# First feed-forward layer: gate and up by the two-matmul product with 512 moving columns, its low half copied out of the bank and added

## The chip, the cores and the metric

One core of a Trainium2 chip runs the whole program. The metric is the device time in microseconds (us) of one execution; lower is better. TensorE is called PE below (PEld its weight loads), VectorE DVE, ScalarE ACT, SyncE SP.

## What is computed

The reference runs 256 tokens (plus 16 meta tokens) of width 1024 through one block of retention and attention with a gated feed-forward layer, and then through two further layers, each with a feed-forward layer of squared ReLU. All weights are fp32 and are read once. The change touches the first feed-forward layer alone:

```
h = h + (silu(n @ w_ffn_gate) * (n @ w_ffn_up)) @ w_ffn_down     # n = rmsnorm(h); 1024 -> 2816 -> 1024
```

The later two (`m0` and `m1` below) are `x + square(relu(h @ w1)) @ w2`, 1024 -> 4096 -> 1024.

## The kernel before, in words

**Number format.** TensorE works on fp32r operands. For accuracy each fp32 operand is split in two parts, hi and lo: ACT writes the hi part of a weight chunk (`whi`, line 1195), DVE subtracts it from the raw chunk and writes the lo part (`wlo`, the `split` of the vector engine, through the helper `tt` at line 1667). A product is then hi·hi + hi·lo + lo·hi. The activations `u` and `v` have the parts as index 0 and 1 of their second dimension.

**Two ways to multiply.** `split_mm` (line 451) gives three matmuls of 256 moving columns for each of the kt = 8 slices of the contraction: whi by u-hi, whi by u-lo, wlo by u-hi, all summed in the same 256 columns of a PSUM bank. `split_wide` (lines 460 and 461) gives two: wlo by u-hi with 256 columns, and whi by both parts of u side by side, 512 columns in one instruction. Then whi by u-lo is summed in the right half of the bank and has to be added to the left half by another engine. Before the change `m0` and `m1` use `split_wide`, and `ffn` uses `split_mm`.

**The stream of weights.** Weights come in chunks of up to 2048 columns into a ring of 4 buffers (`raw`, `whi`, `wlo`). SP loads chunk n once DVE has split chunk n-4 (`lo_ready`). ACT splits chunk n (`hi_ready`) once it has landed and PE has used chunk n-4 (`chunk_used`), DVE follows, PE waits for `lo_ready`. ACT and DVE split three chunks ahead of the one in hand (`AHEAD = 3`).

**The ffn layer.** The hidden width 2816 is cut in 22 steps of 128, k = 0 to 21. A step has an A chunk (gate and up columns of this step, 2 x 1024 columns of a buffer) and a B chunk (128 rows of `w_ffn_down`, 1024 columns). The order on every engine is written out by hand, in `hidden_layer` of each engine's program; k = 1 to 20 run in a hardware loop with two steps in a turn:

- PE: up(0), up(1), down(0), up(2), down(1), ..., up(21), down(20), down(21). `up` (line 889 on) waits for `lo_ready` of its A chunk and for `hidden_val` of step k-2, writes gate and up of the step into two banks of `proj`, and posts `chunk_used`. `down` (line 912) waits for the B chunk and for `hidden_ready` of its own step, and sums into `aux`.
- DVE, for a step k: [split of B chunk k, 1024 columns: wlo] then wait for `chunk_used` of up(k), gate times rms and up times rms/2 (two operations `f<-proj,r_all`, the first posts `ffn_gate_scaled`), wait for `ffn_gate_tanh`, (tanh + 1) times gate (line 1670), times up (`f<-f`, posts `hidden_val`), wait for `hidden_hi`, subtract for the lo part (`v<-f,v`, posts `hidden_ready`), then [split of A chunk k+2, 2048 columns], [split of B chunk k+1], and the next step.
- ACT, for a step k: wait for `ffn_gate_scaled`, tanh (line 1447), wait for `hidden_val`, copy to v-hi (line 1450, posts `hidden_hi`), split of A chunk k+2, split of B chunk k+1 (line 1195).

Every operation of DVE and ACT posts a semaphore for which the engine itself waits before it goes on (`Lane.post` and `Lane.run`), so an engine takes its list strictly in order. In `m0` and `m1` the same list has three more things in a step: ACT first waits for `chunk_used` and copies the right halves of both banks to SBUF (line 1438, `low_kept`), and DVE waits for `low_kept` and adds (`f<-proj,f`, 128x512).

Of the kernel before, what the change touches and what calls it, by code (L numbers as in the profile page):

```python
# [11 lines left out]
P = 128  # L12
# [176 lines left out]
def build(nc, w, params, consts, late, ln_gb, out):  # L189
# [11 lines left out]
    with ExitStack() as ctx:  # L201
# [47 lines left out]
        def W(part, n, off, kt, cols):  # L249

            t = (whi, wlo)[part]
            return t[:, n % RING, off:off + kt * cols].rearrange("p (k n) -> p k n", k=kt)
# [188 lines left out]
        def _(pe):  # L441
# [440 lines left out]
            def hidden_layer(d, norm_no):  # L882
                tag, n_h, kt, k0 = d["tag"], d["n"], d["kt"], d["k0"]
                g = loop_first[tag]
                turn = bank_turn[tag]

                def up(n, k, i=None, gate=None, between=None):
                    pe.wait_ge(sems["lo_ready"], at(lambda m: m + 1, n, i))
                    if k0 + k >= 2:

                        pe.wait_ge(sems["hidden_val"], k0 + k - 1 if i is None else i * 2 + (k0 + k - 1))
                    for j in range(2):
                        first_gate = gate if j == 0 else None
                        if tag == "ffn":
                            ins = split_mm(proj[:, 2 * ((k + turn) % 2) + j, 0:S], lambda a, q: W(a, n, 1024 * j, KT, P)[:, q, :],
                                           lambda a, q: u[:, a, q, META:L], KT, gate=first_gate)
                        else:
                            ins = split_wide(proj[:, 2 * ((k + turn) % 2) + j, :], lambda a, q: W(a, n, 0, KT, 256)[:, q, j * P:(j + 1) * P],
                                           lambda a, q: u[:, a, q, META:L], KT, gate=first_gate)
                        if between and j == 0:  # L900
                            between()
                    finish(ins)

                def down(n, k, i=None, first=False, last=False):
                    pe.wait_ge(sems["lo_ready"], at(lambda m: m + 1, n, i))
                    pe.wait_ge(sems["hidden_ready"], k0 + k + 1 if i is None else i * 2 + (k0 + k + 1))
                    for q in range(kt):
                        for j in range(8):
                            ins = None
                            for s, (a, b) in enumerate(((0, 0), (0, 1), (1, 0))):  # L910

                                ins = mm(aux[:, j // 2, (j % 2) * S:(j % 2 + 1) * S],  # L912
                                         W(a, n, 0, kt, D)[:, q, j * P:(j + 1) * P], v[:, b, 2 * (k % 2) + q, :],
                                         start=first and q == 0 and s == 0 and j % 2 == 0,
                                         stop=last and q == kt - 1 and s == 2, skip_group_check=True)
                            if last and q == kt - 1 and j in (1, 3, 5):
                                ins.then_inc(sems["down_bank"], 1)
                    finish(ins)


                def turn_residual():

                    for k in range(KT):
                        for b in range(2):
                            mm(aux[:, 2 * b + k // 4, (k % 4) * P:(k % 4 + 1) * P], x2[:, k, b * P:(b + 1) * P], C("ident"),
                               start=k % 4 == 0, stop=False, skip_group_check=True)

                def down_tokens(n, k, i=None, last=False):
                    pe.wait_ge(sems["lo_ready"], at(lambda m: m + 1, n, i))
                    pe.wait_ge(sems["hidden_ready"], k0 + k + 1 if i is None else i * 2 + (k0 + k + 1))  # L930
                    for c in range(4):
                        for q in range(kt):
                            for s, (a, b) in enumerate(((0, 0), (0, 1), (1, 0))):
                                ins = mm(aux[:, c, :], v[:, b, 2 * (k % 2) + q, c // 2 * P:(c // 2 + 1) * P],  # L934
                                         W(a, n, 0, kt, D)[:, q, c % 2 * 512:(c % 2 + 1) * 512], start=False,
                                         stop=last and q == kt - 1 and s == 2, skip_group_check=True)
                        if last and c < 3:
                            ins.then_inc(sems["down_bank"], 1)
                    finish(ins)

                pe.wait_ge(sems["proj_free"], order[g - 1])
                up(g, 0, gate=by_half(norm_no), between=lambda: whole_sum(norm_no))
                pe.wait_ge(sems["proj_free"], order[g - 1] + 1)
                up(g + 1, 1)
                pe.wait_ge(sems["rms_ready"], norm_no + 1)
                if tag == "m1":
                    turn_residual()
                    down_tokens(g + 2, 0)
                else:
                    down(g + 2, 0, first=True)  # L950
                add_down = down_tokens if tag == "m1" else down
                with pe.Fori(0, (n_h - 2) // 2) as i:
                    up(g + 3, 2, i)
                    add_down(g + 4, 1, i)
                    up(g + 5, 3, i)
                    add_down(g + 6, 2, i)
                add_down(g + 2 * n_h - 1, n_h - 1, last=True)
# [221 lines left out]
        def _(eng):  # L1179
# [242 lines left out]
            def hidden_layer(d):  # L1422
# [3 lines left out]
                def step(n, k, i=None):  # L1426
# [5 lines left out]
                    if k is None:  # L1432
                        return
                    kk = (lambda c: k0 + k + c if i is None else i * 2 + (k0 + k + c))
                    if tag != "ffn":
                        b = 2 * ((k + bank_turn[tag]) % 2)
                        eng.wait_ge(sems["chunk_used"], at(lambda m: m + 1, n, i))
                        A.post(act(f("f1", 1024, 2, S), proj[:, b:b + 2, S:2 * S], ACT.Copy), "low_kept")  # L1438

                    def buffer_free():  # L1440

# [14 lines left out]
                step(g, 0)  # L1456
                turns = (n_h - 2) // 2
                with eng.Fori(0, turns) as i:
                    A.enter(i, {"hi_ready": 4, "low_kept": 0 if tag == "ffn" else 2, "hidden_hi": 2, "ffn_gate_tanh": 2 if tag == "ffn" else 0})
                    step(g + 1, 1, i)  # L1460
                    step(g + 2, None, i)
                    step(g + 3, 2, i)
                    step(g + 4, None, i)
# [196 lines left out]
        def _(eng):  # L1660
# [390 lines left out]
            def hidden_layer(d, no, gain=None, norm_no=None):  # L2051
# [3 lines left out]
                def step(n, k, i=None):  # L2055
# [7 lines left out]
                    kk = (lambda c: k0 + k + c if i is None else i * 2 + (k0 + k + c))  # L2063
                    eng.wait_ge(sems["chunk_used"], at(lambda m: m + 1, n, i))
                    b, slot = 2 * ((k + bank_turn[tag]) % 2), 2 * (k % 2)
                    if tag == "ffn":
                        g0, hid, up = f("f1", 0, S), f("f1", 256, S), f("f1", 512, S)
                        B.post(tt(g0, proj[:, b, 0:S], rms, ALU.mult), "ffn_gate_scaled")
                        B.run(tt(up, proj[:, b + 1, 0:S], half_rms, ALU.mult))
                        eng.wait_ge(sems["ffn_gate_tanh"], kk(1))  # L2070
                        B.run(stt(g0, proj[:, b, 0:S], 1.0, g0, ALU.add, ALU.mult))
                        B.post(tt(hid, g0, up, ALU.mult), "hidden_val")
                        eng.wait_ge(sems["hidden_hi"], kk(1))
                        B.post(tt(v[:, 1, slot, :], hid, hi32(v[:, 0, slot, :]), ALU.subtract), "hidden_ready")
                    else:
                        rl, hid, both = f("f1", 0, 2, S), f("f1", 512, 2, S), f("f1", 1536, 2, S)
                        eng.wait_ge(sems["low_kept"], kk(1) - M0["k0"])
                        B.run(tt(both, proj[:, b:b + 2, 0:S], f("f1", 1024, 2, S), ALU.add))
                        B.run(stt(rl, both, 0.0, bc(rms, 2), ALU.max, ALU.mult))
                        B.post(tt(hid, rl, rl, ALU.mult), "hidden_val")  # L2080
                        eng.wait_ge(sems["hidden_hi"], kk(1))
                        B.post(tt(v[:, 1, slot:slot + 2, :], hid, hi32(v[:, 0, slot:slot + 2, :]), ALU.subtract), "hidden_ready")
# [3 lines left out]
                step(g, 0)  # L2086
                turns = (n_h - 2) // 2
                with eng.Fori(0, turns) as i:
                    B.enter(i, {"lo_ready": 4, "hidden_val": 2, "hidden_ready": 2, "dve_step": 4,
                                "ffn_gate_scaled": 2 if tag == "ffn" else 0})  # L2090
                    step(g + 1, 1, i)
                    step(g + 2, None, i)
                    step(g + 3, 2, i)
                    step(g + 4, None, i)
# [400 lines left out]
```

## Time and profile before

| what | value |
|---|---|
| runs | 1081.0 us median of 3 (1079.75 to 1083.07) |
| profiled execution, span from first to last instruction | 1076.7 us |
| what lies around the span, against the median | 4.3 us |
| PE busy / PEld busy / DVE busy / ACT busy | 1057.1 / 979.9 / 747.6 / 547.2 us |
| ffn layer in the trace | up(1) starts at 287.7, last `down` starts at 467.6 us |

The profiled execution's own time outside the profiler isn't listed; the 4.3 us are the median of the runs less the span. A PE row's duration is longer than the distance to the next row, since matmuls are pipelined: read the distance of starts. "idle before <-" names what ended an engine's wait.

### The profile page before, as it was taken

The numbers are of one execution on the slowest core, as the hardware profiler recorded it, in microseconds if no ns is written. First come the engines' busy times: TensorE is split into PE (matmuls) and PEld (weight loads), VectorE is DVE, ScalarE is ACT, GpSimd is POOL, SyncE is SP. The second block draws the span as 40 slices with busy tenths as digits, with TensorE's granted clock in tenths as the row PEclk, the third lists the DMA queues.
The fourth block names the chain that finished last, engine by engine and source line by source line (L and its number), as shares of the span: only waits on it lengthen the run. The fifth ranks groups of instructions, "written<-read, shape, count | busy, mean of one in ns | idle before, by whom it ended". The sixth has DMA issues, their size and how long they took to land.

```text
span 1076.7 us, 19451 instructions
## 1 busy us (share of the span) xinstructions
PE 1057.1 (98%) x7774; PEld 979.9 (91%) x7774; DVE 747.6 (69%) x810; ACT 547.2 (51%) x587; POOL 2.2 (0%) x5
## 2 busy tenths in 40 slices
PE   8999999999999999999999999999999999999998
PEld 7998897999999999989989999999999998888887
DVE  6855748768766766677767766666679987666673
ACT  6423536554644444455786444343566574354442
POOL 0000000000000000000000000000000000000000
PEclk9999999999999999999999999999999999999999
DMA  9883243336556556746316564654354454655531
GB/s 308 229 225 118 79 142 100 126 124 194 158 170 200 176 176 191 237 150 202 117 46 230 162 228 156 205 185 135 101 160 154 141 173 157 211 180 183 207 117 39
DMA packets 162589, 177.37 MB, mean 165 GB/s; under 512 B 4800, under 2 KB 148288, under 8 KB 162536
## 3 DMA queue, kind: packets, MB, share of 16 engines
q1 hardware_dynamic: 160704, 174.33, 50.5%
q10 hardware_dynamic: 1832, 2.30, 1.2%
q8 instruction: 38, 0.62, 0.2%
q14 instruction: 15, 0.12, 0.0%
HBM read 175.04 MB, written 1.57 MB: 164 GB/s over the span
## 4 chain that ended last, share of the span: by engine, by line
PE 76%; DVE 16%; ACT 4%; DMA 1%; issue 1%; ACTq 1%; SPq 0%; DVEq 0%
PE proj L451 32%; PE aux L912 13%; PE proj L461 10%; PE aux L934 8%; DVE wlo L1667 6%; PE proj L460 5%; DVE f L1667 3%; DVE f L1670 2%; ACT whi L1195 1%; DMA gamma_rows<-f 1%; DVE u L1670 1%; PE aux L665 1%; PE aux L518 1%; PE aux L780 1%; PE aux L765 1%
## 5 line engine op out<-in xcount | busy, mean ns | idle before, releaser
L1667 DVE TENSOR_TENSOR wlo<-raw,whi 128x2048 fp32r<-128x2048 f32 (+2 forms) x179 | 374.7, 2093 | 113.0 <-ACT whi L1195 101.3
L451 PE MATMUL proj<-u,whi 128*128 128x256 f32 (+1 forms) x1888 | 347.2, 285 | 2.7 <-DVE f L1667 1.6
L1195 ACT ACTIVATE whi<-raw 128x2048 fp32r<-128x2048 f32 (+2 forms) x173 | 309.7, 1790 | 70.7 <-PE proj L451 29.4
L451 PEld LDWEIGHTS proj<-u,whi 128*128 128x128 f32 x1888 | 292.9, 190 | 8.8 <-issue 6.5
L451 PE MATMUL proj<-u,wlo 128*128 128x256 f32 (+1 forms) x944 | 267.1, 283 | 0.0
L461 PE MATMUL proj<-u,whi 128*128 128x512 f32 x512 | 179.9, 393 | 0.0
L451 PEld LDWEIGHTS proj<-u,wlo 128*128 128x128 f32 x944 | 179.3, 190 | 0.0
L912 PE MATMUL aux<-v,whi 128*128 128x256 f32 x864 | 155.2, 281 | 1.8 <-DVE v L1667 1.8
L460 PE MATMUL proj<-u,wlo 128*128 128x256 f32 x512 | 143.6, 281 | 0.9 <-DVE u L1670 0.9
L912 PEld LDWEIGHTS aux<-v,whi 128*128 128x128 f32 x864 | 133.3, 189 | 3.0 <-issue 2.3
L912 PE MATMUL aux<-v,wlo 128*128 128x256 f32 x432 | 121.1, 280 | 0.0
L461 PEld LDWEIGHTS proj<-u,whi 128*128 128x128 f32 x512 | 96.1, 188 | 20.9
L451 PE MATMUL proj<-v,whi 128*128 128x256 f32 (+1 forms) x564 | 103.1, 284 | 0.6 <-DVE f L1667 0.5
L460 PEld LDWEIGHTS proj<-u,wlo 128*128 128x128 f32 x512 | 96.4, 188 | 3.3 <-DVE u L1670 1.4
L451 PEld LDWEIGHTS proj<-v,whi 128*128 128x128 f32 x564 | 87.1, 189 | 2.9 <-issue 2.1
L912 PEld LDWEIGHTS aux<-v,wlo 128*128 128x128 f32 x432 | 81.5, 189 | 0.0
L934 PE MATMUL aux<-whi,v 128*128 128x512 f32 x256 | 80.1, 394 | 0.0
L451 PE MATMUL proj<-v,wlo 128*128 128x256 f32 (+1 forms) x282 | 79.5, 282 | 0.0
L1438 ACT ACTIVATE f<-proj 128x512 f32<-128x512 f32 x32 | 19.1, 598 | 98.3 <-PE proj L461 98.1
L1667 DVE TENSOR_TENSOR f<-proj,r_all 128x256 f32<-128x256 f32 (+5 forms) x85 | 46.4, 545 | 30.9 <-PE proj L451 26.7
L451 PE MATMUL proj<-whi,u 128*128 128x256 f32 (+1 forms) x352 | 65.1, 280 | 1.1 <-DVE f L1673 0.6
L1454 ACT ACTIVATE v<-f 128x512 fp32r<-128x512 f32 x32 | 20.3, 634 | 79.2 <-DVE f L1667 75.2
(302 smaller groups left out, 1092.2 us busy)
## 6 DMA issues: line engine op xcount, KB each, us to landing
raw<-in_mlp_w_dram SPq DMA_DIRECT2D x64, 1024.0 KB, 5.5
raw<-in_w_in_dram SPq DMA_DIRECT2D x21, 1024.0 KB, 7.1
raw<-in_od_w_in_dram SPq DMA_DIRECT2D x12, 1024.0 KB, 5.5
raw<-in_w_ffn_gate_dram SPq DMA_DIRECT2D x22, 512.0 KB, 4.0
raw<-in_w_ffn_up_dram SPq DMA_DIRECT2D x22, 512.0 KB, 5.2
raw<-in_w_ffn_down_dram SPq DMA_DIRECT2D x21, 512.0 KB, 5.4
raw<-in_ev_w_in_dram SPq DMA_DIRECT2D x10, 1024.0 KB, 6.1
raw<-in_w_ret_out_dram SPq DMA_DIRECT2D x4, 1024.0 KB, 5.2
```

Of the source, the lines that this page charges most:

```text
L451: ins = mm(o, w_of(a, k), x_of(b, k), start=first and k == 0 and j == 0, stop=last and k == kt - 1 and j == 2, skip_group_check=skip)
L460: mm(bank[:, 0:S], w_of(1, k), x_of(0, k), start=k == 0, stop=False, skip_group_check=True)
L461: ins = mm(bank, w_of(0, k), x_of(slice(0, 2), k), start=False, stop=k == kt - 1, skip_group_check=True)
L518: ins = mm(aux[:, 0, 0:tokens], weights, sq_of(tokens)[:, k, :], start=k == 0, stop=k == KT - 1, skip_group_check=True)
L665: ins = mm(out[e], rv_tok[:, 1 - j, h * P:(h + 1) * P], sd[:, e, j, :], start=False, stop=j == 1)
L912: ins = mm(aux[:, j // 2, (j % 2) * S:(j % 2 + 1) * S], W(a, n, 0, kt, D)[:, q, j * P:(j + 1) * P], v[:, b, 2 * (k % 2) + q, :], start=fir ...
L934: ins = mm(aux[:, c, :], v[:, b, 2 * (k % 2) + q, c // 2 * P:(c // 2 + 1) * P], W(a, n, 0, kt, D)[:, q, c % 2 * 512:(c % 2 + 1) * 512], st ...
L1195: A.post(act(whi[:, n % RING, 0:wd], raw[:, n % RING, 0:wd], ACT.Copy), "hi_ready")
L1438: A.post(act(f("f1", 1024, 2, S), proj[:, b:b + 2, S:2 * S], ACT.Copy), "low_kept")
L1454: A.post(act(v[:, 0, 2 * (k % 2):2 * (k % 2) + 2, :], f("f1", 512, 2, S), ACT.Copy), "hidden_hi")
L1667: return ve.tensor_tensor(o, a, b, op)
L1670: return ve.scalar_tensor_tensor(out=o, in0=a, scalar=s, in1=b, op0=op0, op1=op1)
```

## The change

In `hidden_layer` of PE, ffn's gate and up now go through `split_wide` as well, with the same weight chunks in the same places. ACT copies the right halves of both banks to SBUF in every step of ffn too, ahead of tanh, and waits for `chunk_used` ahead of that. DVE adds left half and copy (128x512) ahead of the scaling, which then reads the sum in SBUF in place of the bank. The loop's tables of semaphore counts follow, and the wait of m0 and m1 for `low_kept` counts ffn's 22 posts as well.

```diff
@@ PE, up @@
                     for j in range(2):
                         first_gate = gate if j == 0 else None
-                        if tag == "ffn":
-                            ins = split_mm(proj[:, 2 * ((k + turn) % 2) + j, 0:S], lambda a, q: W(a, n, 1024 * j, KT, P)[:, q, :],
-                                           lambda a, q: u[:, a, q, META:L], KT, gate=first_gate)
-                        else:
-                            ins = split_wide(proj[:, 2 * ((k + turn) % 2) + j, :], lambda a, q: W(a, n, 0, KT, 256)[:, q, j * P:(j + 1) * P],
-                                           lambda a, q: u[:, a, q, META:L], KT, gate=first_gate)
+                        def rows_of(a, q):
+                            if tag == "ffn":
+                                return W(a, n, 1024 * j, KT, P)[:, q, :]
+                            return W(a, n, 0, KT, 256)[:, q, j * P:(j + 1) * P]
+
+                        ins = split_wide(proj[:, 2 * ((k + turn) % 2) + j, :], rows_of, lambda a, q: u[:, a, q, META:L], KT,
+                                         gate=first_gate)
@@ ACT, hidden_layer @@
-                    if tag != "ffn":
-                        b = 2 * ((k + bank_turn[tag]) % 2)
-                        eng.wait_ge(sems["chunk_used"], at(lambda m: m + 1, n, i))
-                        A.post(act(f("f1", 1024, 2, S), proj[:, b:b + 2, S:2 * S], ACT.Copy), "low_kept")
+                    b = 2 * ((k + bank_turn[tag]) % 2)
+                    eng.wait_ge(sems["chunk_used"], at(lambda m: m + 1, n, i))
+                    A.post(act(f("f1", 1024, 2, S), proj[:, b:b + 2, S:2 * S], ACT.Copy), "low_kept")
@@ DVE, hidden_layer @@
                     eng.wait_ge(sems["chunk_used"], at(lambda m: m + 1, n, i))
                     b, slot = 2 * ((k + bank_turn[tag]) % 2), 2 * (k % 2)
+                    both = f("f1", 1536, 2, S)
+                    eng.wait_ge(sems["low_kept"], kk(1))
+                    B.run(tt(both, proj[:, b:b + 2, 0:S], f("f1", 1024, 2, S), ALU.add))
                     if tag == "ffn":
                         g0, hid, up = f("f1", 0, S), f("f1", 256, S), f("f1", 512, S)
-                        B.post(tt(g0, proj[:, b, 0:S], rms, ALU.mult), "ffn_gate_scaled")
-                        B.run(tt(up, proj[:, b + 1, 0:S], half_rms, ALU.mult))
+                        B.post(tt(g0, both[:, 0], rms, ALU.mult), "ffn_gate_scaled")
+                        B.run(tt(up, both[:, 1], half_rms, ALU.mult))
                         eng.wait_ge(sems["ffn_gate_tanh"], kk(1))
                         ...
                     else:
-                        rl, hid, both = f("f1", 0, 2, S), f("f1", 512, 2, S), f("f1", 1536, 2, S)
-                        eng.wait_ge(sems["low_kept"], kk(1) - M0["k0"])
-                        B.run(tt(both, proj[:, b:b + 2, 0:S], f("f1", 1024, 2, S), ALU.add))
+                        rl, hid = f("f1", 0, 2, S), f("f1", 512, 2, S)
```

## Rows read from the trace of the kernel before

**Rows 1.** The page, part 1: busy us (share of the span) x instructions

```profile
PE 1057.1 (98%) x7774; PEld 979.9 (91%) x7774; DVE 747.6 (69%) x810; ACT 547.2 (51%) x587; POOL 2.2 (0%) x5
```

**Rows 2.** Chain that ended last, in order of time (start, us, what), ffn

```profile
304.69 5.66 PE proj L451 x48
...
310.35 2.83 PE aux L912 x24
313.18 5.68 PE proj L451 x48
```

**Rows 3.** The same chain in m0, two neighbouring steps

```profile
630.18 5.70 PE aux L912 x48
641.46 5.70 PE aux L912 x48
```

**Rows 4.** Busy by stretch, the middle of ffn; then granted clock and DMA

```profile
295.00:455.00 160.00, 160.00 (x1358) 160.00 (x1357) 107.40 (x134) 71.96 (x76) 0.00 (x0) 1.00 0.63 188
```

**Rows 5.** Timeline of DVE, two steps of ffn (start, us, ..., idle before)

```profile
360.71 1.22 DVE L1667 TENSOR_TENSOR wlo<-raw,whi 128x1024 fp32r<-128x1024 f32 x1 [0.38 <-DVE wlo L1667]
362.06 0.88 DVE L1667 TENSOR_TENSOR f<-proj,r_all 128x256 f32<-128x256 f32 x2
...
366.53 3.64 DVE L1667 TENSOR_TENSOR wlo<-raw,whi 128x2048 fp32r<-128x2048 f32 x2 [1.61 <-ACT whi L1195]
370.30 0.88 DVE L1667 TENSOR_TENSOR f<-proj,r_all 128x256 f32<-128x256 f32 x2
...
378.79 0.88 DVE L1667 TENSOR_TENSOR f<-proj,r_all 128x256 f32<-128x256 f32 x2
```

**Rows 6.** Timeline of ACT, the first of these steps

```profile
362.52 0.39 ACT L1447 ACTIVATE proj<-f 128x256 f32<-128x256 f32 x1 [2.93 <-DVE f L1667]
...
364.58 1.92 ACT L1195 ACTIVATE whi<-raw 128x2048 fp32r<-128x2048 f32 x1 [0.19 <-ACT v L1450]
366.68 1.06 ACT L1195 ACTIVATE whi<-raw 128x1024 fp32r<-128x1024 f32 x1 [0.18 <-ACT whi L1195]
```

**Rows 7.** Waits within ffn, 284 to 468 us (in total, times, longest)

```profile
DVE wlo L1667 <- ACT whi L1195: 33.0, 21, 1.6
...
PE aux L912 <- DVE v L1667: 1.4, 1, 1.4
DVE f L1667 <- PE proj L451: 1.4, 4, 0.4
```

**Rows 8.** Timeline of ACT, then of DVE, one step of m0

```profile
641.50 0.60 ACT L1438 ACTIVATE f<-proj 128x512 f32<-128x512 f32 x1 [3.54 <-PE proj L461]
...
642.13 0.69 DVE L1667 TENSOR_TENSOR f<-proj,f 128x512 f32<-128x512 f32 x1 [1.48 <-ACT f L1438]
642.85 0.69 DVE L1670 SCALAR_TENSOR_TENSOR f<-f,r_all 128x512 f32<-128x512 f32 x1
```

**Rows 9.** Timelines of DVE and ACT at the start of ffn

```profile
289.96 0.88 DVE L1667 TENSOR_TENSOR f<-proj,r_all 128x256 f32<-128x256 f32 x2
...
295.12 0.89 DVE L1667 TENSOR_TENSOR f<-proj,r_all 128x256 f32<-128x256 f32 x2
...
299.60 3.64 DVE L1667 TENSOR_TENSOR wlo<-raw,whi 128x2048 fp32r<-128x2048 f32 x2 [1.61 <-ACT whi L1195]
...
288.67 0.20 ACT L1208 ACTIVATE small<-small 128x1 f32<-128x1 f32 x1
```

**Rows 10.** Timeline of DVE at the end of ffn

```profile
454.85 0.88 DVE L1667 TENSOR_TENSOR f<-proj,r_all 128x256 f32<-128x256 f32 x2 [0.39 <-PE proj L451]
...
464.51 0.88 DVE L1667 TENSOR_TENSOR f<-proj,r_all 128x256 f32<-128x256 f32 x2
...
467.00 0.42 DVE L1667 TENSOR_TENSOR v<-f,v 128x256 fp32r<-128x256 f32 x1 [0.60 <-ACT v L1450]
```

**Rows 11.** Timeline of DVE, the product of gate and up, operands in SBUF

```profile
363.47 0.43 DVE L1667 TENSOR_TENSOR f<-f 128x256 f32<-128x256 f32 x1
```

**Rows 12.** Timeline of PE, and busy by stretch, at the start of the program

```profile
10.04 1.13 PE L574 MATMUL proj<-cst,f 128*128 128x128 f32 x6 [1.90 <-DMA f<-in_x_dram]
...
12.00:14.00 2.00, 2.00 (x10) 1.87 (x10) 1.86 (x5) 1.77 (x3) 0.00 (x0) 0.50 1.11 350
```

More of the change, by code:

```diff
@@ L1458, in hidden_layer @@
                 with eng.Fori(0, turns) as i:
-                    A.enter(i, {"hi_ready": 4, "low_kept": 0 if tag == "ffn" else 2, "hidden_hi": 2, "ffn_gate_tanh": 2 if tag == "ffn" else 0})
+                    A.enter(i, {"hi_ready": 4, "low_kept": 2, "hidden_hi": 2, "ffn_gate_tanh": 2 if tag == "ffn" else 0})
                     step(g + 1, 1, i)
@@ L2088, in hidden_layer @@
                 with eng.Fori(0, turns) as i:
-                    B.enter(i, {"lo_ready": 4, "hidden_val": 2, "hidden_ready": 2, "dve_step": 4,
+                    B.enter(i, {"lo_ready": 4, "hidden_val": 2, "hidden_ready": 2, "dve_step": 6 if tag == "ffn" else 4,
                                 "ffn_gate_scaled": 2 if tag == "ffn" else 0})
```

## The prediction, made before the changed kernel was run

> **What bounds the kernel now.** The page's first part comes first: PE is busy for 98% of the span, DVE for 69%, ACT for 51% [rows 1]. Taken alone it says that only PE counts. The stretch in question has to be read by itself, and by its period rather than by busy time. In the chain of waits ffn is a steady alternation of up (48 matmuls, 5.68 us) and down (24, 2.83 us), 8.51 us a step [rows 2]; from 295 to 455 us PE is busy for all of 160 us [rows 4]. So PE is the bound there before.
>
> The second thing to read is how far behind PE the other two engines run. Take DVE in the same stretch and measure from one scaling of the gate to the next: 362.06 to 370.30 is 8.24 us, 370.30 to 378.79 is 8.49 us [rows 5] (the second has the jump back of the hardware loop, with 0.38 us idle before its wlo). Neither start shows a wait for PE. What sets them is a ring through two engines, whose links follow at once on one another: gate scaled at 362.06, tanh on ACT at 362.52, copy to v, then ACT's 2048-column split at 364.58 [rows 6], then DVE's two lo splits from 366.53 to 370.17, then the next gate at 370.30 [rows 5]. DVE has 1.61 us idle in it, and ACT 2.93, but both idle times lie inside the ring: DVE waits for a split that ACT may start only after tanh and the copy, since ACT works its list in order. The ring turns in 16.73 us for two steps, 8.37 a step, against PE's 8.51. **Its slack is 0.14 us a step, though DVE is busy for only two thirds of the time.** The waits confirm it: DVE waited for up of PE only 4 times in 22 steps, 1.4 us in all, longest 0.4 [rows 7]; it began the layer late and only caught up near its end. At the end PE waits 1.4 us for the last v [rows 7].
>
> **The change, part by part.**
>
> *PE.* Each up has 32 matmuls and weight loads where it had 48, for the same 768 columns a slice. m0 has this form: from one down to the next is 641.46 - 630.18 = 11.28 us, less the down's 5.70, leaves 5.58 for its up of the same size [rows 3], against 5.68 [rows 2]. That is 0.10 us a step, 2.2 us over 22 steps, and a PE period of 8.41. It counts only while PE is the bound.
>
> *ACT.* One copy of 128x512 from PSUM in each step, 0.60 us [rows 8], and a wait for chunk_used ahead of it, with tanh, the copy to v and two splits queued behind. Its place is the idle time before tanh: ACT ends its 1024-column split at 366.68 + 1.06 = 367.74, and tanh of the next step can't start before the next gate is scaled, about 370.7 [rows 5, 6]. The copy can start when up(k) is done. DVE is going to fall behind PE (below), so up(k) is then long done, and the copy is over before DVE asks. I cost it at nothing; its cover is those 2.93 us, and if PE ended its up last, the copy would be in series: 0.63 us a step with the hand-over (641.50 to 642.13 [rows 8]). In step 0 ACT is free at 288.87 and DVE scales at 289.96 [rows 9], which just holds a copy of 0.60.
>
> *DVE.* One addition of 128x512 of a bank and SBUF ahead of the gate's scaling: m0 has the same operation, 0.69 us, and the next starts 0.73 us (642.85 - 642.13, rounded up) after it [rows 8]. It lies in the ring, nothing covers it. The wait for low_kept costs nothing where the copy is done; one more wait that has passed already I bound by 0 and 0.1 us a step (the gap of 0.13 from the end of wlo to the gate [rows 5] has one), and take 0.
>
> *The scalings* read the sum in SBUF in place of the bank. A product of two SBUF operands of 128x256 takes 0.43 us [rows 11], a pair of scalings out of the bank 0.88 [rows 5]: no difference, so I take 0. The Trainium skill (VectorE: DVE Perf Modes, the section on the TRN2 errata) has a fixed term of 58 cycles for an SBUF source and 120 for PSUM, which by its 0.96 GHz would be an estimated 0.065 us less for the gate's link, 1.4 us over the layer. By it the sum below would be 13.8; the rows show none of it, and the sum goes by the rows.
>
> *The sum.* With the addition the ring is 16.73 + 2 x 0.73 = 18.19 us for two steps, 9.10 a step: longer than PE's 8.41. The bound changes hands. What counts now is the ring from its first to its last link, and before it also ran nearly unhindered: gate(0) at 289.96, gate(20) at 454.85, gate(21) at 464.51 [rows 9, 10]. So all 22 additions go onto the end of the layer, 22 x 0.73 = 16.1 us, less what DVE spent waiting for PE: 1.4 us in 4 times [rows 7], less the 0.13 that stand before each gate anyway, about 0.9. **The last v comes 15.2 us later, at about 482.6 in place of 467.4** [rows 10]. PE's 2.2 us are hidden in its waits. A check from PE's side: the lo split of A chunk 3 ends at 299.60 + 2.29 = 301.9 for an up that starts at 304.69 [rows 2, 9], a lead of 2.8; minus the 1.46 of two additions and 0.3 of faster ups, about 1 us is left, and each step eats 9.10 - 8.41 = 0.69. From the third step on PE waits for wlo some 0.7 us a step, 17 times, about 12 us; at the end down(20) is over about 7.2 us before the last v (it was 1.4). 12 + (7.2 - 1.4) - 2.2 gives 15.6, the same within my rounding.
>
> *After the layer* everything hangs on that v (residual, norm, next projections), and the splits that ACT and DVE do ahead there are in the same lists, so they shift along. SP, its loads and the later layers are unchanged but for the count they wait for. I count no recovery.
>
> *The clock.* The wait of 7.2 us is longer than any in the trace before. There PE idled 1.90 us at 8.1 to 10.0 us, and after it the granted clock was 0.50 of full, the 1.2 GHz level, from 12 to 14 us [rows 12]. The 1.4 us at the end of ffn had no such trace. So I expect the last down and what follows it to start at half clock. Priced from those rows: 10 matmuls in 2 us, 0.20 each, against 0.118 at full clock (2.83 over 24 [rows 2]) is 0.08 lost on each. I don't know how many will be slow; for 10 to 16 it is 0.8 to 1.3 us. Part of it may hide behind DVE's residual additions, so the bounds are 0.6 and 1.3, and I take 1.0. The Trainium skill (TensorE: Matmul & The Clock Gate, on what is actually happening) says that an idle array falls to 1.2 GHz and regains 2.4 by activity; that speaks for this case.
>
> Sum: 15.2 + 1.0 = 16.2 on the profiled span of 1076.7, 1092.9 with 4.3 us around it: against the median **1081.0 + 16.2 = 1097.2 us**.
>
> **The rivals.**
> - *No fall of the clock:* 1081.0 + 15.2 = 1096.2. The same in all else. Chance 0.33.
> - *PE stays the bound, not slower:* the Trainium skill (Perfetto Trace Analysis, the section on the most-contended engine) says to improve the most occupied engine first, and that is PE, at 98%. The mechanism here would be that DVE's 1.61 us of idle time absorb the 0.73: ACT's split would have to be ready earlier. Then only the 2.2 us count: 1081.0 - 2.2 = 1078.8, too little to tell from no change (about 0.3%, 3.2 us, is what a measurement of this kernel can). It decides at a ring of 8.41 us: for more than 0.04 us of addition the ring loses. Against it: the 21 waits of wlo for ACT [rows 7] follow at once upon ACT's own end [rows 6]. Chance 0.05: 0.03 for this, and 0.02 for more than 3.2 us faster, should PE gain at the layer's end as well.
> - *Copy and addition both in series:* 22 x 0.63 = 13.9 more, 1111. It needs PE's up to end last in each step, which a ring slower than PE excludes. Chance 0.04.
> - *Partly absorbed:* the ring has slack that I don't see (the hardware loop's 0.38 us taken up by the longer step, the skill's cheaper SBUF source): 10 x 0.25 + 1.4, about 4 less, 1092 to 1093. Chance 0.08.
>
> **How the numbers follow.** The forecast's own case has 0.47, and its range goes from 1095.5 to 1099.5 (the wait at 0.1 us a step gives 2.2 on top of it, the clock 0.6 to 1.3). The range with the neighbours is 1092.5 to 1100; outside lie PE as the bound, the series case and 0.03 for what I haven't thought of (0.02 of it no change, 0.01 faster), under 0.2 together. Slower by over 0.3%: 0.47 + 0.33 + 0.04 + 0.08 = 0.92; within: 0.03 + 0.02 = 0.05; faster: 0.02 + 0.01 = 0.03.
>
> **What would show it.** Right: gates 9.0 to 9.2 us apart on DVE; no wait of DVE for up of PE or for the copy after the first steps; PE waits of about 0.7 us for wlo in most steps and one of about 7 us for the last v, and DVE the same 1.6 us for ACT; up at 5.6 us where PE doesn't wait; the last v near 482.6; a clock under 1 shortly after. Wrong: a period near 8.4 with PE busy throughout (the ring had slack), a period near 9.7 with DVE waiting for ACT's copy (the copy is in the ring), or a shift at the end of ffn that has shrunk by the end of the program (the later stages had room).

## The result and the profile after

The changed kernel took 1099.8 us (median of 4 runs, 1098.9 to 1100.9) where the kernel before took 1081.4 beside it. The ratio of the runs is 1.0183, with a 95% interval of 1.0166 to 1.0201: slower by about 1.8%, 18.4 us by the medians and 19.8 by the ratio. The prediction was 1097.2 with a range up to 1100.0; by the ratio the kernel comes out at 1100.8, so the direction and the ring as the bound were right and the size fell short by 2.6 to 3.6 us.

The span of the profiled execution went from 1076.7 to 1097.2, 20.5 us. Not all of that is the change: the two executions differ by 1.3 us before ffn begins. DVE's reciprocal at the layer's start stands at 285.52 before and at 286.82 after; already the PE work at 10.04 that waits for a part of the input [rows 12] starts at 10.33, and in the other profiled executions below the reciprocal stands anywhere from 285.3 to 288.0. So from here on I measure **the stretch**: from this reciprocal to the start of the last `v` of ffn (a), and to the reciprocal of the next norm (b), which takes in what follows the layer. Before, (a) is 467.00 - 285.52 = 181.48 and (b) is 480.72 - 285.52 = 195.20. The changed kernel and two runs below that should have the same ring give 200.08, 200.05 and 200.13 for (a), so a few tenths of a microsecond in it can be read. The first part of the page, and the kinds of wait within ffn, after:

The page, part 1:

```profile
PE 1062.6 (97%) x7422; PEld 967.5 (88%) x7422; DVE 762.7 (70%) x832; ACT 560.3 (51%) x609; POOL 2.2 (0%) x5
```

The waits within 284 to 490 us (in total, times, longest), kernel after:

```profile
DVE wlo L1667 <- ACT whi L1196: 31.3, 21, 1.6
...
DVE v L1667 <- ACT v L1450: 14.6, 22, 1.0
PE proj L460 <- DVE wlo L1667: 10.0, 16, 0.8
...
PE aux L913 <- DVE v L1667: 7.2, 2, 6.7
...
DVE wlo L1667 <- DVE wlo L1667: 4.9, 10, 0.6
DVE f L1667 <- DVE wlo L1667: 4.3, 20, 0.2
```

PE has 352 matmuls fewer (22 x 16), and waits where it did not: 16 times for the lo split of a chunk, 10 us, and 6.7 us for the last v. In [rows 7] its only wait was the last, 1.4. DVE's waits for up have vanished from the list, and DVE doesn't wait for ACT's copy in it either. DVE's busy share rose by one point only, 69% to 70%: no share of busy time says what happened here.

Two steps in the same places of the loop's body as in [rows 5] (steps 3 and 4, there 9 and 10), with the addition of step 2 ahead of them. DVE's timeline after, and under it ACT's for step 3 (start, us, ..., idle before):

```profile
306.34 0.69 DVE L1667 TENSOR_TENSOR f<-proj,f 128x512 f32<-128x512 f32 x1 [0.21 <-DVE wlo L1667]
...
315.88 0.69 DVE L1667 TENSOR_TENSOR f<-proj,f 128x512 f32<-128x512 f32 x1 [0.22 <-DVE wlo L1667]
316.60 0.89 DVE L1667 TENSOR_TENSOR f<-f,r_all 128x256 f32<-128x256 f32 x2
...
319.10 0.43 DVE L1667 TENSOR_TENSOR v<-f,v 128x256 fp32r<-128x256 f32 x1 [0.60 <-ACT v L1450]
321.12 3.64 DVE L1667 TENSOR_TENSOR wlo<-raw,whi 128x2048 fp32r<-128x2048 f32 x2 [1.59 <-ACT whi L1196]
324.97 0.69 DVE L1667 TENSOR_TENSOR f<-proj,f 128x512 f32<-128x512 f32 x1 [0.21 <-DVE wlo L1667]
```

```profile
312.11 1.06 ACT L1196 ACTIVATE whi<-raw 128x1024 fp32r<-128x1024 f32 x1 [0.57 <-PE proj L461]
313.29 0.60 ACT L1438 ACTIVATE f<-proj 128x512 f32<-128x512 f32 x1
317.12 0.39 ACT L1447 ACTIVATE proj<-f 128x256 f32<-128x256 f32 x1 [3.24 <-DVE f L1667]
```

Read them with the ring in mind. The copy at 313.29 is over at 313.89, 2 us before DVE adds: it is covered. The addition at 315.88 has nothing before it but wlo, so it isn't. And three small links have grown: 0.21 to 0.22 us between wlo and the addition, where 0.13 stood before the scaling; (not shown) 0.52 to 0.57 in the jump of the hardware loop, where 0.38 to 0.40 stood; and from the start of the gate's scaling to the start of tanh, 316.60 to 317.12, it is 0.52 us, where 362.06 to 362.52 [rows 5, 6] was 0.46. From addition to addition over two steps, 306.34 to 324.97, are 18.63 us (18.58 from the third turn of the loop on); the sum had 18.19, and before it was 16.73.

The end of the layer, DVE and then PE:

```profile
481.36 2.29 DVE L1667 TENSOR_TENSOR wlo<-raw,whi 128x2048 fp32r<-128x2048 f32 x1 [0.21 <-DVE wlo L1667]
483.69 0.69 DVE L1667 TENSOR_TENSOR f<-proj,f 128x512 f32<-128x512 f32 x1
...
486.90 0.42 DVE L1667 TENSOR_TENSOR v<-f,v 128x256 fp32r<-128x256 f32 x1 [0.60 <-ACT v L1450]
489.20 0.69 DVE L1667 TENSOR_TENSOR x_all<-x_all,aux 128x512 f32<-128x512 f32 x1 [1.87 <-PE aux L913]
```

```profile
487.48 0.76 PE L913 MATMUL aux<-v,whi 128*128 128x256 f32 x2 [6.68 <-DVE v L1667]
```

Stretch (a) is 486.90 - 286.82 = 200.08, which is 18.6 more than before, and (b) 214.49, 19.3 more. The difference between the two, 0.7, is put down to the clock (tried below). Busy time by stretch (PE, PEld, DVE, ACT, POOL, then the granted clock, DMA share and GB/s):

```profile
482.00:484.00 2.00, 0.00 (x0) 0.00 (x0) 1.97 (x2) 0.00 (x0) 0.00 (x0) 1.00 0.75 242
484.00:486.00 2.00, 0.00 (x0) 0.00 (x0) 1.77 (x5) 0.39 (x1) 0.00 (x0) 1.00 1.09 371
486.00:488.00 2.00, 0.53 (x2) 0.56 (x3) 0.73 (x2) 1.60 (x2) 0.00 (x0) 0.51 1.10 349
488.00:490.00 2.00, 2.00 (x12) 2.00 (x11) 0.69 (x1) 0.33 (x3) 0.00 (x0) 0.50 0.28 87
490.00:492.00 2.00, 2.00 (x11) 2.00 (x11) 1.45 (x3) 1.90 (x4) 0.00 (x0) 0.50 0.00 0
```

The clock is at 1.2 GHz (0.50) when the last down begins, at 487.48.

### The profile page after: what moved, and what is told of

The parts are those of the page before. It is cut to its first block, busy times and chain, and to the rows that moved or that the text cites. A ratio compares the mean times of both kernels' runs of the same rounds, so it can differ in the third digit from the quotient of the medians.

```text
span 1097.2 us, 18797 instructions
## 1 busy us (share of the span) xinstructions
PE 1062.6 (97%) x7422; PEld 967.5 (88%) x7422; DVE 762.7 (70%) x832; ACT 560.3 (51%) x609; POOL 2.2 (0%) x5
## 4 chain that ended last, share of the span: by engine, by line
PE 61%; DVE 24%; ACT 9%; issue 3%; DMA 2%; ACTq 1%; DVEq 0%; SPq 0%
PE proj L451 21%; DVE wlo L1667 12%; PE proj L461 10%; PE aux L913 9%; PE aux L935 8%; DVE f L1667 6%; PE proj L460 5%; ACT whi L1196 5%; DVE f L1670 3%; DMA gamma_rows<-f 1%; ACT v L1450 1%; ACT proj L1447 1%; PE aux L665 1%; PE aux L518 1%; PE aux L780 1%
## 5 line engine op out<-in xcount | busy, mean ns | idle before, releaser
L461 PE MATMUL proj<-u,whi 128*128 128x512 f32 x864 | 303.5, 393 | 0.0
L460 PE MATMUL proj<-u,wlo 128*128 128x256 f32 x864 | 244.1, 282 | 11.1 <-DVE wlo L1667 10.0
L451 PE MATMUL proj<-u,whi 128*128 128x256 f32 (+2 forms) x1184 | 222.2, 289 | 1.9 <-DVE f L1667 1.6
L461 PEld LDWEIGHTS proj<-u,whi 128*128 128x128 f32 x864 | 162.3, 188 | 34.9
L451 PEld LDWEIGHTS proj<-u,whi 128*128 128x128 f32 (+1 forms) x1184 | 186.2, 192 | 6.4 <-issue 5.4
L460 PEld LDWEIGHTS proj<-u,wlo 128*128 128x128 f32 x864 | 162.6, 188 | 17.7 <-DVE wlo L1667 8.0
L451 PE MATMUL proj<-u,wlo 128*128 128x256 f32 (+2 forms) x592 | 168.8, 285 | 0.0
L451 PEld LDWEIGHTS proj<-u,wlo 128*128 128x128 f32 (+1 forms) x592 | 113.4, 192 | 0.0
L1438 ACT ACTIVATE f<-proj 128x512 f32<-128x512 f32 x54 | 32.3, 598 | 99.3 <-PE proj L461 96.8
L1667 DVE TENSOR_TENSOR f<-proj,f 128x512 f32<-128x512 f32 x54 | 37.3, 692 | 46.5 <-ACT f L1438 41.2
```

What stands on the lines that cost most here:

```text
L451: ins = mm(o, w_of(a, k), x_of(b, k), start=first and k == 0 and j == 0, stop=last and k == kt - 1 and j == 2, skip_group_check=skip)
L460: mm(bank[:, 0:S], w_of(1, k), x_of(0, k), start=k == 0, stop=False, skip_group_check=True)
L461: ins = mm(bank, w_of(0, k), x_of(slice(0, 2), k), start=False, stop=k == kt - 1, skip_group_check=True)
L1667: return ve.tensor_tensor(o, a, b, op)
```

## The experiments

Theory 1, the prediction's: a ring through DVE and ACT (scaling, tanh, product, copy to v, ACT's split of the next A chunk, DVE's two splits) sets ffn's period, the addition lies in it, PE's saving and ACT's copy don't. The rivals: the wide product costs PE time; ACT's copy is on the path; DVE has too much work. Each ratio is to executions of the kernel before on the same chip; the runs stood on more than one chip, so compare ratios or stretches across rows, and not medians. (a) and (b) are from each run's one profile.

| run | median us | ratio to before, 95% | (a) us | (b) us |
|---|---|---|---|---|
| kernel before | | 1 | 181.48 | 195.20 |
| changed kernel | 1099.8 | 1.0183 (1.0166 to 1.0201) | 200.08 | 214.49 |
| PE part alone | 1079.2 | 1.0000 (0.9987 to 1.0013) | 180.48 | 194.88 |
| ACT and DVE part alone | 1100.2 | 1.0195 (1.0182 to 1.0208) | 200.05 | 214.45 |
| ACT's split first | 1083.6 | 1.0039 (1.0026 to 1.0052) | 182.64 | 197.04 |
| before, ACT's split first | 1080.2 | 1.0002 (0.9993 to 1.0012) | 181.57 | 195.30 |
| no second wait | 1098.0 | 1.0188 (1.0166 to 1.0210) | 198.37 | 212.79 |
| half addition | 1093.2 | 1.0132 (1.0117 to 1.0147) | 194.25 | 208.66 |
| copy twice | 1101.9 | 1.0194 (1.0177 to 1.0211) | 200.44 | 214.86 |
| array kept busy | 1100.2 | 1.0198 (1.0183 to 1.0213) | 200.13 | 213.90 |
| split first, peeled | 1080.7 | 1.0001 (0.9985 to 1.0017) | 180.71 | 194.82 |
| the same, next split late | 1079.2 | 0.9988 (0.9976 to 0.9999) | 180.49 | 195.39 |
| before, peeled | 1080.0 | 1.0007 (0.9992 to 1.0022) | 180.37 | 194.11 |

**PE's part alone.** In the kernel before, PE's part of the diff and nothing else.

```diff
-                        if tag == "ffn":
-                            ins = split_mm(proj[:, 2 * ((k + turn) % 2) + j, 0:S], ...)
+                        ins = split_wide(proj[:, 2 * ((k + turn) % 2) + j, :], rows_of, lambda a, q: u[:, a, q, META:L], KT,
+                                         gate=first_gate)
```

> The kernel before with only TensorE's part of the change in ffn: the two-matmul product, without ACT's copy and DVE's addition. Left out of the computation: the products of the hi weights with the lo activations of gate and up (they lie unread in the banks' right halves). Theory 1 (a ring through ACT and DVE sets the period): the ring stays at 8.37 us a step and PE comes to 8.41, so 0.5 to 2.5 us faster than the kernel before, 1079 to 1081. Theory 2 (the wide product itself costs PE time, part of the 18 to 20 us): slower than before by several us.

Ratio 1.0000, stretch (a) 1.0 shorter. The wide product costs nothing: theory 2 falls. It gives nearly nothing either. The ring at 8.37 was only just below PE's 8.51, and now it is the ring that holds: the gates stand 8.22 to 8.24 and 8.48 to 8.51 us apart to the end of the loop. And of the 1.0 us stretch (b) keeps only 0.3, since after PE's longer wait at the end the clock is at half here too (0.50 from 468 to 470 us; (b) less (a) is 14.40 as in the changed kernel, before 13.72). In the waits of this run DVE no longer waits for PE and still waits 33.0 us for ACT's split, while PE's last wait has grown from 1.4 to 2.5:

```profile
DVE wlo L1668 <- ACT whi L1196: 33.0, 21, 1.6
...
PE aux L913 <- DVE v L1668: 2.5, 1, 2.5
```

**ACT's and DVE's part alone.** The changed kernel with `split_mm` on PE again, and the copy from the left halves:

```diff
-                    A.post(act(f("f1", 1024, 2, S), proj[:, b:b + 2, S:2 * S], ACT.Copy), "low_kept")
+                    A.post(act(f("f1", 1024, 2, S), proj[:, b:b + 2, 0:S] if tag == "ffn" else proj[:, b:b + 2, S:2 * S], ACT.Copy), "low_kept")
```

> The changed kernel with TensorE's old three-matmul product in ffn; ACT copies the banks' left halves (the right ones are not written) and DVE adds them. The computation is changed thereby: gate and up come out doubled. Theory 1: within 1 us of the changed kernel, 18 to 20 us slower than before, since PE's 2.2 us are hidden. Theory 2: near the kernel before.

Stretch (a) is 200.05 against 200.08: the whole slowdown without any of PE's part, and PE's 2.2 us are hidden in its waits.

**How the addition counts, and the copy.** Two runs change one length each:

```diff
 half addition, DVE:
+                    if tag == "ffn":
+                        B.run(tt(both[:, 0], proj[:, b, 0:S], f("f1", 1024, S), ALU.add))
...
-                        B.run(tt(up, both[:, 1], half_rms, ALU.mult))
+                        B.run(tt(up, proj[:, b + 1, 0:S], half_rms, ALU.mult))
 copy twice, ACT:
+                    if tag == "ffn":
+                        A.run(act(f("f1", 1024, 2, S), proj[:, b:b + 2, S:2 * S], ACT.Copy))
                     A.post(act(f("f1", 1024, 2, S), proj[:, b:b + 2, S:2 * S], ACT.Copy), "low_kept")
```

> The changed kernel, DVE adds the low sums of gate alone (128x256 in place of 128x512); up is scaled out of its bank. Left out of the computation: up's products of hi weights with lo activations. Ring theory: the link is 0.43 in place of 0.69 us, 22 x 0.27 = 5.8 us less than the changed kernel, stretch about 194.3. Rival (a fixed cost of an extra instruction or wait makes the slowdown, not its length): no or little change.

Stretch 194.25, expected 194.3: an addition that is 0.27 us shorter takes 5.8 us off 22 steps. DVE's rows in this run, where the half addition takes 0.42 to 0.43 us:

```profile
351.07 0.42 DVE L1667 TENSOR_TENSOR f<-proj,f 128x256 f32<-128x256 f32 x1 [0.22 <-DVE wlo L1667]
351.53 0.43 DVE L1667 TENSOR_TENSOR f<-f,r_all 128x256 f32<-128x256 f32 x1
351.99 0.42 DVE L1667 TENSOR_TENSOR f<-proj,r_all 128x256 f32<-128x256 f32 x1
```

They answer the question of the source for the duration of a scaling: out of SBUF (351.53) and out of the bank (351.99) it differs by nothing that counts. The hand-over from the gate's scaling to tanh is another matter: it is 0.52 us in this run too.

> The changed kernel, ACT does its copy twice in each ffn step. Ring theory: ACT has over 3 us idle there, the second copy ends before DVE asks: within 1 us of the changed kernel. Rival (the copy is on the path): 0.6 us a step, 13 us slower than the changed kernel.

The second copy adds 22 x 0.63 = 13.9 us to ACT's list and 0.36 us to the stretch. The run's own executions differ (1096.9 to 1106.1), but its ratio agrees with that of the changed kernel within both intervals. ACT's rows show both copies and 2.6 us of idle time still behind them:

```profile
351.64 0.60 ACT L1439 ACTIVATE f<-proj 128x512 f32<-128x512 f32 x1
352.27 0.60 ACT L1440 ACTIVATE f<-proj 128x512 f32<-128x512 f32 x1
355.48 0.39 ACT L1449 ACTIVATE proj<-f 128x256 f32<-128x256 f32 x1 [2.61 <-DVE f L1669]
```

**What the sum left out.** 3.4 us of the 18.6 in stretch (a) aren't in the 15.2. One candidate is DVE's second wait ahead of the addition:

```diff
-                    eng.wait_ge(sems["chunk_used"], at(lambda m: m + 1, n, i))
+                    if tag != "ffn":
+                        eng.wait_ge(sems["chunk_used"], at(lambda m: m + 1, n, i))
```

> The changed kernel without DVE's own wait for chunk_used of up(k) in ffn (its wait for low_kept covers it, since ACT waits for chunk_used before the copy). Theory 1a (each wait of DVE costs time in the ring even where it has passed, about 0.09 us): the gap between wlo and the addition falls from 0.21 to about 0.13, 22 x 0.09 = 2 us less than the changed kernel, and the layer's stretch from the reciprocal to the last v falls from 200.1 to about 198. Theory 1b (a passed wait is free and the extra 3.4 us of the stretch are something else): no change.

The stretch falls by 1.71 us, and the addition follows wlo at 360.66, 0.12 after its end, where 0.21 stood:

```profile
356.90 3.64 DVE L1667 TENSOR_TENSOR wlo<-raw,whi 128x2048 fp32r<-128x2048 f32 x2 [1.59 <-ACT whi L1196]
360.66 0.69 DVE L1667 TENSOR_TENSOR f<-proj,f 128x512 f32<-128x512 f32 x1
...
368.70 1.23 DVE L1667 TENSOR_TENSOR wlo<-raw,whi 128x1024 fp32r<-128x1024 f32 x1 [0.52 <-DVE wlo L1667]
```

By the ratios alone (1.0188 and 1.0183) this couldn't be told; the stretch tells it. The cost belongs to the loop: in step 21, which stands behind it, the split ends at 481.36 + 2.29 = 483.65 and the addition starts at 483.69, 0.04 later with both waits in between. Inside the loop a wait's count is worked out from the number of the turn, outside it is a constant; whether that makes the difference I didn't try.

The rest is in DVE's rows. Between one wlo and the next, at the jump of the loop and behind its last turn, DVE was idle 4.0 us in 10 times before and 4.9 after. Nine jumps back grew from 0.38 to 0.40 us each to 0.52 to 0.57, and the gap behind the last turn shrank from 0.57 to 0.21. That is 0.9 us together. The waits and the last of these splits before:

```profile
DVE wlo L1667 <- DVE wlo L1667: 4.0, 10, 0.6
```

```profile
462.18 2.29 DVE L1667 TENSOR_TENSOR wlo<-raw,whi 128x2048 fp32r<-128x2048 f32 x1 [0.57 <-DVE wlo L1667]
```

(Those of after stand above.) The later start of tanh gives 1.1 us: the gaps from the second scaling to the operation that needs tanh add up to 1.62 us before and 2.75 after. The two waits for ACT that follow, for v-hi and for the split, are 0.3 us less. 16.1 - 0.9 + 1.7 + 0.9 + 1.1 - 0.3 = 18.6, the whole. Why the jump got longer (DVE has one operation more in each half of the loop's body; without the second wait it is 0.52 as well), and why tanh starts later, stays open. Tanh's 0.52 us isn't simply the addition's doing: in the kernel before, steps 0 and 21, which stand outside the loop, have 0.51 to 0.52 as well.

**The clock.** In the changed kernel PE gets work for its wait:

```diff
+                if tag == "ffn":
+                    pe.wait_ge(sems["hidden_val"], k0 + n_h - 1)
+                    pe.wait_ge(sems["lo_ready"], g + 2 * n_h)
+                    for _ in range(27):
+                        mm(proj[:, 2 * ((n_h - 2 + turn) % 2), :], W(0, g + 2 * n_h - 1, 0, kt, D)[:, 0, 0:P],
+                           u[:, 0:2, 0, META:L], start=True, stop=True, skip_group_check=True)
                 add_down(g + 2 * n_h - 1, n_h - 1, last=True)
```

> The changed kernel, with 27 matmuls of 512 columns added before ffn's last down, into two banks' halves that nobody reads, in the 6.7 us in which PE waits. Nothing of the result changes. Clock theory: the granted clock stays at 1.00 over the wait, the last down runs at full clock, the residual additions start 0.5 us sooner after the last v, and the whole is 0.5 to 1.3 us faster than the changed kernel. Rival (the matmuls after the wait are off the path anyway): no change beyond 0.3 us.

The profile shows what was expected: the clock stays at 1.00, the first residual addition comes 1.65 us after the last v's start in place of 2.30, and (b) less (a) is 13.77 in place of 14.41, before 13.72.

```profile
479.81 6.44 PE L962 MATMUL proj<-u,whi 128*128 128x512 f32 x27 [0.51 <-DVE wlo L1673]
```

```profile
484.00:486.00 2.00, 2.00 (x10) 1.54 (x9) 1.21 (x3) 1.08 (x2) 0.00 (x0) 1.00 1.10 350
486.00:488.00 2.00, 2.00 (x19) 2.00 (x18) 0.90 (x2) 0.98 (x3) 0.00 (x0) 1.00 0.51 159
```

So the half clock costs 0.65 us here, of 1.0 that I took (slightly more, since the added matmuls end late: the last down starts 0.67 us after v, where it was 0.58). The runs don't show it (ratios 1.0198 and 1.0183, intervals of 0.15 to 0.18% to either side): it is too small for them, and that the whole gets faster, as expected, isn't shown.

**Breaking the ring.** No work is removed, ACT only does the split of A chunk k+2 ahead of step k's copy, tanh and v, as soon as up(k) is done:

```diff
 ACT, step():
                     if i is not None:
-                        split(n + AHEAD, i)
+                        if tag != "ffn" or k is not None:
+                            split(n + AHEAD, i)
+                        if tag == "ffn" and k is not None:
+                            split(n + 1 + AHEAD, i)
```

> The changed kernel, ACT's order in ffn changed: the split of A chunk k+2 stands ahead of step k's own copy, tanh and copy to v, in place of behind them. No work is added or removed. Theory 1: the link from tanh over the copy to v to ACT's split to DVE's split is gone, DVE's 1.6 us of waiting for ACT go, the ring is under 8.41, PE is the bound again: 1078.5 to 1080.5, faster than both. Rival (DVE has too much work in a step, or ACT's copy is on the path): stays over 1090.

> The kernel before with the same order of ACT. Theory 1: PE was the bound already, only the late start of DVE and the wait at the layer's end can shrink: 0 to 1.5 us faster than before. Rival: if the order helps by itself, apart from the addition, it gains as much here as in the changed kernel (some 20 us).

By the ratios 1.44 of the 1.83% are back, 15.6 us, and by stretch (a) 17.4 of the 18.6 us, with DVE's work unchanged: it isn't the amount of work but its order. The same order does nothing for the kernel before (1.0002), where the ring wasn't the bound. DVE's timeline in the changed kernel with ACT's split first:

```profile
352.95 3.64 DVE L1670 TENSOR_TENSOR wlo<-raw,whi 128x2048 fp32r<-128x2048 f32 x2
357.59 0.69 DVE L1670 TENSOR_TENSOR f<-proj,f 128x512 f32<-128x512 f32 x1 [1.00 <-ACT f L1441]
...
364.28 1.23 DVE L1670 TENSOR_TENSOR wlo<-raw,whi 128x1024 fp32r<-128x1024 f32 x1 [0.52 <-DVE wlo L1670]
365.98 0.69 DVE L1670 TENSOR_TENSOR f<-proj,f 128x512 f32<-128x512 f32 x1 [0.47 <-ACT f L1441]
```

wlo no longer waits for ACT (the 1.6 us are gone); DVE waits for the copy, thus for PE. From 357.59 to 449.98 are 11 steps of 8.40 us, PE's period with the wide product, 0.11 below the 8.51 of before: this is PE's saving, seen at last. The expectation was still missed: 1083.6 and not 1078.5 to 1080.5. I had priced the steady steps and not the end. The new order puts ACT's split in front of the copy, so the addition starts 2.6 us after PE is through with a step's up. PE covers that while it has further steps, but not at the end: up(20) is over at 455.8, the addition of step 20 starts at 458.39, and that of step 21 at 467.09, behind two 2048-column splits in DVE's list. PE then waits 3.9 us for v, with half clock afterwards (0.50 from 472 to 476 us).

```profile
455.81 1.92 ACT L1196 ACTIVATE whi<-raw 128x2048 fp32r<-128x2048 f32 x1 [1.46 <-PE proj L461]
457.76 0.60 ACT L1441 ACTIVATE f<-proj 128x512 f32<-128x512 f32 x1
```

In stretch (b) this is 1.8 us more than before; the ratio says 4.2 (2.8 at the low end of its interval), and no stretch shows where the rest lies.

Three more runs looked at the end. The first two have ACT's split first and are without DVE's second wait; the third is the kernel before with the last turn written out and nothing else. On ACT and DVE the last turn of ffn's loop is written out, so that the last B chunk is split at its own 1024 columns (in the loop it gets the width of an A chunk), and in the second of them DVE does step 21 ahead of the next stage's first split:

```diff
-                turns = (n_h - 2) // 2
+                turns = (n_h - 2) // 2 - (tag == "ffn")
...
+                if tag == "ffn":
+                    m = g + 1 + 4 * turns
+                    step(m, n_h - 3)
+                    step(m + 1, None)
+                    step(m + 2, n_h - 2)
+                    step(m + 3, None)
                 pump(g + 2 * n_h - 3)
                 step(g + 2 * n_h - 3, n_h - 1)
```

> The changed kernel with ACT's split ahead of the step's chain, without DVE's second wait, and with the last turn of ffn's hardware loop written out on ACT and DVE, so that the last B chunk is split at its own 1024 columns (in the loop it has the width of an A chunk, 2048). Ring theory, where the end of the layer is what is left: DVE's chain of step 21 starts 1.07 us sooner than with the split first alone, stretch about 181.5 (182.6 there), the whole about 1 us faster than it, 1082 to 1083; still not faster than the kernel before, whose stretch is 181.5. Rival (something other than the end of the layer holds the last 3.6 us): unchanged.

> As split_first_peeled, and DVE does its chain of step 21 ahead of the lo split of the first chunk of the next stage (before, behind it). The last v comes about 1.2 us sooner still, stretch about 180.3, but the split then stands between it and the residual additions: these start 2.7 us after the last v in place of 2.3. Whole: 0 to 1 us faster than split_first_peeled, within 1 us of the kernel before.

> The kernel before with the last loop turn of ffn written out on ACT and DVE alone. DVE's chain of step 21 waits for the second 2048-column split until 464.5 though PE's up is done at 463.4: 0.9 us can be gained, stretch about 180.6, whole 0.5 to 1 us faster than before, at the edge of what can be measured.

Peeling, with the second wait left out, takes 1.9 us off stretch (a) of the version with ACT's split first (1.1 expected) and the whole to 1.0001 of the kernel before (1080.7 us, where 1082 to 1083 was expected). All of it is gained at the end: measured from the reciprocal, the addition of step 18 stands at 153.92 and 153.90 us in the two versions, that of step 20 at 170.72 and 170.00, that of step 21 at 179.42 and 177.50. What held the last few us was the end of the layer; how the 1.9 us divide between the narrower split, the second wait and the jump that is no more, this run doesn't tell. Doing the next split late shortens (a) by another 0.2 only (1.2 expected) and lengthens (b) by 0.6, as the split then stands before the residual additions:

```profile
468.26 2.29 DVE L1676 TENSOR_TENSOR wlo<-raw,whi 128x2048 fp32r<-128x2048 f32 x1
470.59 1.41 DVE L1676 TENSOR_TENSOR x_all<-x_all,aux 128x512 f32<-128x512 f32 x2
```

Its ratio, 0.9988 with 0.9999 as the interval's end, is just below one, but its stretch (b) is 0.2 us longer than before's: the 1.0 us that it saves up to the last v is spent again ahead of the next norm. So I don't call it faster. The kernel before, peeled, has both stretches 1.1 us shorter (0.9 expected), and the runs don't resolve it (1.0007). **No version here beats the kernel before by more than 0.3%**; the changed one with ACT's split first and the end peeled equals it.

## Why the prediction came out as it did

- *What bounds the kernel:* right. The ring of 8.37 us, with 0.14 us a step of slack beneath a PE that is busy all the time, is what the order experiment breaks up, and the period goes from 9.29 back to 8.40 us a step.
- *PE's part:* right, 0.10 us a step (0.11 measured where PE is the bound) and wholly hidden: 200.05 without it, 200.08 with it.
- *ACT's copy at nothing:* right, 0.36 us for a second one in all 22 steps.
- *The addition at 0.73 us, 22 times:* right; its length counts one for one (5.8 us for 0.27 a step).
- *The scalings at nothing:* right for their duration, by the rows at 351.53 and 351.99, but not for the link that hangs on them (below). The 1.4 us estimated from the figures of the Trainium skill (VectorE: DVE Perf Modes, the TRN2 errata) don't appear: in this case the duration of a tensor_tensor of 128x256 is the same from SBUF and from the bank.
- *The waits of PE:* 16 for wlo, 10.0 us, expected 17 and about 12; 6.7 us at the end, expected 7.2.
- ***The step that failed:*** the ring's new period was the old one plus the addition and nothing else, 18.19 us for two steps; it measured 18.58 to 18.63. The term that was mis-sized is "one more wait that has passed already I bound by 0 and 0.1 us a step ... and take 0". It measured 0.09 us in each of the loop's 20 steps, and 1.7 us of the stretch, within the bound but at its far end: this wait lay in the ring. Two terms the sum didn't have at all: the hardware loop's jump, counted at its old length, 0.9 us more over the layer, and the hand-over from the gate's scaling to tanh, 0.06 us longer in a step of the loop, 1.1 us. The two waits for ACT gave 0.3 back. Together these are the 3.4 us that were missing in the ring. What makes the last two longer is open.
- *The range:* 1095.5 to 1099.5 isn't what the terms named beside it add up to: 1081.0 + 15.2 + 0.6 is 1096.8, and 1081.0 + 15.2 + 2.2 + 1.3 is 1099.7. It had 2.2 us for the wait and nothing for the jump and for tanh, and the 3.4 us took the time past the wider range's 1100 too, by the ratio.
- *The clock:* right in kind, and the Trainium skill's rule (TensorE: Matmul & The Clock Gate) agrees: 0.50 when the last down begins, back at 1.00 by 494 us, and no fall when PE is kept busy. 0.65 us where I took 1.0. That the fall comes with the wait is shown, and its price by the stretch; the runs are too coarse for it. The 2.5 us of waiting in the run with PE's part alone were followed by 0.50 too.
- *The rivals:* "PE stays the bound", 1078.8, is what the rule to improve the most occupied engine first stood for (the Trainium skill, Perfetto Trace Analysis, on the most-contended engine). Here it failed: that engine got 2.2 us less to do and the kernel 1.8% slower. It holds for the period once the ring is broken, 8.40 us, and even then the end of the layer gives the gain back.
- *The 4.3 us around the span:* after the change, time and span of the profiled execution are 1098.9 and 1097.2, 1.7 apart. With the same 1.7 the profiled execution of before took an estimated 1078.4, some 2.6 us less than the median. Profile against profile the shift looks like 20.5; stretch (b), which leaves out the start of the program, says 19.3, and the ratio 19.8.

## What to carry to other kernels

Before adding work to an engine that is idle a third of the time, measure from one of its repeated operations to the next and find what each idle time inside waits for: where the waits close on themselves through a second engine's ordered list, the idle time is no cover, and the slack is the bound's period less the ring's. In a ring count everything, also a wait that has long been fulfilled, the jump of the loop and each hand-over between engines: here 0.73 us of addition a step came with 0.2 us of such things. And a ring is often cheaper to break by the order of one engine's list than by taking work out, but then price the end of the loop by itself, since the last step has no successor to hide it.

## What I had not expected of the hardware

- In the hardware loop a further DVE wait on a semaphore that is already fulfilled cost 0.09 us: 0.21 us from wlo to the addition with two waits, 0.12 with one. Outside the loop the same place had 0.04 us with both.
- The gap in DVE's list across the hardware loop's jump back was 0.38 to 0.40 us with seven operations in a step, and 0.52 to 0.57 with eight, also with the extra wait taken out (0.52). Behind the loop's last turn it was the other way round, 0.57 and 0.21.
- Tanh on ACT started 0.46 us after the start of the scaling that it waits for in the loop of the kernel before, and 0.52 us in the loop of the changed one.
- 6.7 us of idle PE were followed by a granted clock of 0.50, which cost the following stretch 0.65 us; 2.5 us (PE's part alone) were followed by 0.50 as well, and the 1.4 us of before left it at 1.00.
